# Five matmuls per fp32r weight tile in the feed-forward, in place of six

## What is computed

```python
def rmsnorm(x, g):
    y = xf * lax.rsqrt(jnp.mean(xf * xf, axis=-1, keepdims=True) + EPS)
    return (y * g).astype(x.dtype)

def swiglu(h, w_gu, w_down):
    gate, up = jnp.split(h @ w_gu, 2, axis=-1)
    return (jax.nn.silu(gate) * up) @ w_down

def layer(...):
    x = x + 0.5 * swiglu(rmsnorm(x, n1), ffn1_gu, ffn1_down)
    h = rmsnorm(x, n_mix)
    ...            # projections, gated linear attention and window attention
    x = x + jnp.concatenate([o_g, o_s], axis=-1) @ w_out
    x = x + 0.5 * swiglu(rmsnorm(x, n2), ffn2_gu, ffn2_down)
```

## Time and profile before

| | |
|---|---|
| median of 3 runs | 2183.99 us (2182.62 to 2188.75) |
| span of the profiled execution | 2178.1 us |
| what lies between the two | 5.9 us |
| TensorE matmul busy | 2116.3 us, 97% |
| VectorE, ScalarE, GpSimd busy | 811.9, 581.5, 800.7 us |

### The profile page before, as it was taken

One profiled execution on the slowest core, in us unless ns is written; L12 is line 12 of the kernel. 1 busy time (PEld: TensorE's weight loads), 2 busy tenths in 40 slices (PEclk: granted clock), 3 DMA queues, 4 the chain that ended last, 5 costly groups with the idle time before them and its releaser, 6 DMA issues.

```text
span 2178.1 us, 40378 instructions
## 1 busy us (share of the span) xinstructions
PE 2116.3 (97%) x16718; PEld 2078.8 (95%) x16718; DVE 811.9 (37%) x1125; ACT 581.5 (27%) x795; POOL 800.7 (37%) x337
## 2 busy tenths in 40 slices
PE   6999999999999999999999999999999999999996
PEld 6999999998889999999999999999898999999996
DVE  5222222486257222222332222226754452222224
ACT  3222222235233222222232222222532322222222
POOL 3333344432113333344433333444221233444443
PEclk9999999999889999999999999999997999999998
DMA  4222222421212222222222222233221122222222
GB/s 137 90 87 87 87 87 97 132 78 50 81 51 78 87 88 88 88 93 97 89 87 87 87 88 88 96 96 123 69 90 39 61 88 87 87 87 87 92 92 99
DMA packets 56869, 190.53 MB, mean 87 GB/s; under 512 B 8976, under 2 KB 10672, under 8 KB 56240
## 3 DMA queue, kind: packets, MB, share of 16 engines
q1 hardware_dynamic: 48960, 176.31, 25.0%
q10 hardware_dynamic: 7824, 13.00, 1.8%
HBM read 184.37 MB, written 6.95 MB: 88 GB/s over the span
## 4 chain that ended last, share of the span: by engine, by line
PE 92%; DVE 6%; issue 1%; ACT 0%; DMA 0%; DVEq 0%; ACTq 0%
PE ps L379 84%; DVE h_hi L989 2%; PE ps L538 1%; DVE ssum L1003 1%; PE ps L651 1%; PE ps L527 1%; DVE h_lo L992 1%; PE ps L444 1%; PE ps L645 1%; PE ps L690 1%; PE ps L718 0%; PE ps L510 0%; DVE x L1323 0%; PE ps L679 0%; PE ps L704 0%
## 5 line engine op out<-in xcount | busy, mean ns | idle before, releaser
L366 POOL TENSOR_TENSOR w_lo<-w_raw,w_hi 128x1024 fp32r<-128x1024 f32 x332 | 800.3, 2411 | 1359.4 <-ACT w_hi L745 1345.2
L379 PE MATMUL ps<-h_hi,w_hi 128*128 128x272 f32 x3424 | 718.8, 291 | 23.8 <-DVE h_lo L992 22.1
L379 PE MATMUL ps<-h_lo,w_hi 128*128 128x272 f32 x3424 | 712.9, 290 | 0.0
L379 PE MATMUL ps<-h_hi,w_lo 128*128 128x272 f32 x3424 | 710.8, 289 | 0.0
L745 ACT ACTIVATE w_hi<-w_raw 128x1024 fp32r<-128x1024 f32 x328 | 347.5, 1060 | 1349.2 <-PE ps L379 1349.1
L379 PEld LDWEIGHTS ps<-h_hi,w_hi 128*128 128x128 f32 x3424 | 544.1, 190 | 28.8 <-issue 24.8
L379 PEld LDWEIGHTS ps<-h_hi,w_lo 128*128 128x128 f32 x3424 | 543.4, 190 | 0.0
L379 PEld LDWEIGHTS ps<-h_lo,w_hi 128*128 128x128 f32 x3424 | 538.9, 190 | 0.0
L379 PE MATMUL ps<-act_lo,w_hi 128*128 128x272 f32 x1408 | 291.6, 289 | 0.0
L379 PE MATMUL ps<-act_hi,w_hi 128*128 128x272 f32 x1408 | 291.2, 288 | 0.0
L379 PE MATMUL ps<-act_hi,w_lo 128*128 128x272 f32 x1408 | 290.4, 288 | 0.0
(11 more groups left out here) (213 smaller groups left out, 1246.8 us busy)
## 6 DMA issues: line engine op xcount, KB each, us to landing
w_raw<-stream SPq DMA_DIRECT2D x332, 512.0 KB, 3.4
x<-xT ACTq DMA_DIRECT2D x8, 272.0 KB, 6.3
y_d<-x SPq DMA_DIRECT2D x8, 272.0 KB, 2.1
s<-s_d ACTq DMA_DIRECT2D x2, 1024.0 KB, 4.9
s_s_d<-s ACTq DMA_DIRECT2D x2, 1024.0 KB, 4.6
kc<-kc_d ACTq DMA_DIRECT2D x2, 512.0 KB, 5.2
vc<-vc_d ACTq DMA_DIRECT2D x2, 512.0 KB, 6.6
k_s_d<-kc_d ACTq DMA_DIRECT2D x2, 496.0 KB, 8.9
```

The costliest lines, as they stand in the source:

```text
L366: pool.tensor_tensor(w_lo[:, q, :], w_raw[:, q % RAW, :], w_hi[:, q, :].bitcast(F32), ALU.subtract).then_inc(lo_ready, 1)
L379: ins = pe.matmul(dst[:, hf, :], w[:, slot, cols], r[:, hf * TH:(hf + 1) * TH], start=first and w is w_hi and r is rhs_hi, stop=last and r ...
```

## The change

In the feed-forward alone, the moving operand of a weight tile is laid out as one row of 1088 columns: high half 0, the first 90 low columns of half 0, high half 1, the first 90 low columns of half 1, and the other 2 x 182 low columns. `wide_product` runs w_hi over it in three matmuls of 362, 362 and 364 columns, and w_lo over the two high halves in two of 272. The three w_hi matmuls write three PSUM banks (a `tri`), with the low products beside the high ones; they are added on the way out. So an output tile takes three banks and only two are in the air (six banks; the last two serve the norm). The evacuation becomes: ScalarE copies the low columns out (`copy_low`, two instructions), VectorE adds the high columns (`add_high`), then scales in SBUF. ScalarE also makes the high part of h (`high_h`) and of act (`high_act`). The head of a feed-forward half is written anew: the first two tiles run over seven k, then their last k, then `norm_sum`, then the third tile, which needs the first tile's banks.

```diff
+TAIL = 90
+REST = TH - TAIL
+HW = TH + TAIL
+TW = 2 * T
...
+        def tri(i):
+            return ps[:, 3 * i:3 * i + 3, :]
...
+            def wide_product(dst, slot, col, r, first, last):
+
+                cols = slice(col, col + P)
+                for hf in range(2):
+                    pe.matmul(dst[:, hf, 0:HW], w_hi[:, slot, cols], r[:, hf * HW:(hf + 1) * HW],
+                              start=first, stop=False)
+                pe.matmul(dst[:, 2, 0:2 * REST], w_hi[:, slot, cols], r[:, 2 * HW:TW], start=first, stop=last)
+                for hf in range(2):
+                    ins = pe.matmul(dst[:, hf, 0:TH], w_lo[:, slot, cols], r[:, hf * HW:hf * HW + TH],
+                                    start=False, stop=last)
+                return ins
...
-                pe.wait_ge(h_ready, hb + 5)
-                for q in range(4):
-                    if q == 3:
-                        pe.wait_ge(norm_root, l * 3 + (half * 2 + 1))
-                    model_tile(pair(q), ch + q, q, hb if q == 0 else None).then_inc(chunk_done, 1)
-                    if q == 0:
-                        norm_sum(l * 3 + half * 2)
+                pe.wait_ge(h_ready, hb + (1 if half == 0 else 6))
+                pe.wait_ge(down_used, l * (2 * KT) + (half * KT + 1))
+                for q in range(2):
+                    pe.wait_ge(lo_ready, ch + (q + 1 + RING))
+                    if q:
+                        pe.wait_ge(h_ready, hb + (KT - 1))
+                        pe.wait_ge(down_used, l * (2 * KT) + (half * KT + 2))
+                    for k in range(KT - 1):
+                        if q == 0:
+                            pe.wait_ge(h_ready, hb + (k + 1))
+                        wide_product(tri(q), q, k * P, hx[:, k, :], k == 0, False)
+                pe.wait_ge(h_ready, hb + KT)
+                for q in range(2):
+                    wide_product(tri(q), q, (KT - 1) * P, hx[:, KT - 1, :], False, True).then_inc(chunk_done, 1)
+                norm_sum(l * 3 + half * 2, 3)
+                for q in range(2):
+                    pe.wait_ge(up_used if q else gate_summed, fb + 1)
+                    wide_tile(tri(q), ch + (2 + q), 2 + q).then_inc(chunk_done, 1)
...
+            def high_h(n, gain, wide):
+
+                act.activation(high_cols(hx[:, n, :]) if wide else mid_cols(hx[:, n, :])[0],
+                               halves(x[:, n, :]), ACT.Copy, scale=gain).then_inc(h_high, 1)
+
+            def copy_low(dst, src, done):
+
+                act.wait_ge(chunk_done, done + 1)
+                d = low_pieces(dst)
+                act.activation(d[0], src[:, 0:2, TH:HW], ACT.Copy)
+                act.activation(d[1], halves(src[:, 2, 0:2 * REST]), ACT.Copy).then_inc(low_copied, 1)
...
-                high_part(chunk(l, c0 + RING), 0)
-                root(l * 3 + half * 2)
-                for q in range(1, 4):
-                    high_part(chunk(l, c0 + RING + q), q)
+                for q in range(4):
+                    c = chunk(l, c0 + RING + q)
+                    copy_low((a_buf if q % 2 else g_buf)[:, q // 2, :], tri(q % 2), c[0])
+                    high_part(c, q)
+                    if q == 1:
+                        root(l * 3 + half * 2)
+                        silu(fb, 0)
+                    elif q == 2:
+                        silu(fb + 1, 1)
                     if q % 2:
-                        silu(fb + q // 2, q // 2)
+                        high_act(fb + q // 2, q // 2, q // 2)
...
+            def add_high(dst, src, count):
+
+                dve.wait_ge(low_copied, count)
+                return dve.tensor_tensor(halves(dst), src[:, 0:2, 0:TH], halves(dst), ALU.add)
...
                 scale_ready(l * 3 + half * 2)
                 with dve.Fori(0, FT // 2) as i:
                     for q in range(2):
+                        dve.wait_ge(chunk_done, i * 4 + (cb + 2 * q + 1 + RING))
+                        add_high(g_buf[:, q, :], tri(0), i * 4 + (wb + 2 * q + 1)).then_inc(gate_summed, 1)
+                        dve.wait_ge(gate_summed, i * 2 + (fb + q + 1))
                         if q == 0:
                             dve.wait_ge(rs_ready, l * 3 + (half * 2 + 1))
...
                 def evacuate(n):
                     dve.wait_ge(chunk_done, cb + (CH_GU + DN_CH * (n + 1) + RING))
-
-                    dve.scalar_tensor_tensor(out=halves(a_buf[:, n % 2, :]), in0=pair(n % 4), scalar=0.5,
-                                             in1=halves(rs[:, :]), op0=ALU.mult,
-                                             op1=ALU.mult).then_inc(down_used, 1)
-                    dve.wait_ge(down_used, l * (2 * KT) + (half * KT + n + 1 + 4))
+                    add_high(a_buf[:, n % 2, :], tri(n % 2), wb + CH_GU + n + 1).then_inc(down_used, 1)
+                    dve.wait_ge(down_used, l * (2 * KT) + (half * KT + n + 1 + 2))
+
+                    dve.scalar_tensor_tensor(out=a_buf[:, n % 2, :], in0=a_buf[:, n % 2, :], scalar=0.5,
+                                             in1=rs[:, :], op0=ALU.mult, op1=ALU.mult).then_inc(down_scaled, 1)
+                    dve.wait_ge(down_scaled, l * (2 * KT) + (half * KT + n + 1))
                     dve.tensor_tensor(x[:, n, :], x[:, n, :], a_buf[:, n % 2, :], ALU.add).then_inc(x_ready, 1)
```

More of the change, by code:

```diff
@@ L258, in pair, with high_cols, low_cols, mid_cols @@
             return ps[:, 2 * i:2 * i + 2, 0:TH]
+        def tri(i):
+            return ps[:, 3 * i:3 * i + 3, :]
+        def high_cols(ap):
+            return ap[:, 0:2 * HW].rearrange("p (h n) -> p h n", h=2)[:, :, 0:TH]
+        def low_cols(ap):
+            return (ap[:, 0:2 * HW].rearrange("p (h n) -> p h n", h=2)[:, :, TH:HW],
+                    ap[:, 2 * HW:TW].rearrange("p (h n) -> p h n", h=2))
+        def mid_cols(ap):
+            q = ap.rearrange("p (h c n) -> p h c n", h=2, c=2)
+            return q[:, :, 0, :], q[:, :, 1, :]
+        def low_pieces(ap):
+            two = ap if len(ap.shape) == 3 else halves(ap)
+            return two[:, :, 0:TAIL], two[:, :, TAIL:TH]
         def halves(ap):
@@ L387, in model_tile, with wide_tile, norm_sum @@
                 for k in range(KT):
-                    if hb is not None and k >= 5:
+                    if hb is not None and k >= 7:
                         pe.wait_ge(h_ready, hb + (k + 1))
-                    ins = product(dst, slot, k * P, h_hi[:, k, :], h_lo[:, k, :], k == 0, k == KT - 1)
+                    ins = product(dst, slot, k * P, *mid_cols(hx[:, k, :]), k == 0, k == KT - 1)
                 return ins
-            def norm_sum(phase):
+            def wide_tile(dst, chunk, slot):
+                pe.wait_ge(lo_ready, chunk + (1 + RING))
+                for k in range(KT):
+                    ins = wide_product(dst, slot, k * P, hx[:, k, :], k == 0, k == KT - 1)
+                return ins
+            def norm_sum(phase, at):
                 pe.wait_ge(ssum_ready, phase + 1)
-                square_sum(pair(3), ssum).then_inc(norm_summed, 1)
+                square_sum(pair(at), ssum).then_inc(norm_summed, 1)
             def ffn_half(l, half):
@@ L436, in output_half @@
                         pe.wait_ge(m["mix_ready"], half * 4 + k + 1)
-                    ins = product(dst, c % RING, (n % 2 * 4 + k) * P, *mixed(half * 4 + k),
+                    ins = product(dst, c % RING, (n % 2 * 4 + k) * P, *map(halves, mixed(half * 4 + k)),
                                   k == 0, k == 3)
@@ L983, in rope_swap, with new_h @@
                 return [8 + i if i < 8 else i - 8 if i < 16 else i for i in range(32)]
-            def new_h(n, gain, step, squares):
-                dve.tensor_scalar(h_hi[:, n, :], x[:, n, :], gain, None, ALU.mult).then_inc(h_step, 1)
-                k = n + max(n - 2, 0) + 1
-                dve.wait_ge(h_step, step + k)
-                dve.scalar_tensor_tensor(out=h_lo[:, n, :], in0=x[:, n, :], scalar=gain,
-                                         in1=h_hi[:, n, :].bitcast(F32), op0=ALU.mult,
-                                         op1=ALU.subtract).then_inc(h_ready, 1)
+            def new_h(n, gain, wide, adds, squares):
+                dve.wait_ge(h_high, squares + n + 1)
+                his = low_pieces(high_cols(hx[:, n, :]).bitcast(F32)) if wide else \
+                    (mid_cols(hx[:, n, :])[0].bitcast(F32),)
+                los = low_cols(hx[:, n, :]) if wide else (mid_cols(hx[:, n, :])[1],)
+                xs = low_pieces(x[:, n, :]) if wide else (halves(x[:, n, :]),)
+                for lo, hi, src in zip(los, his, xs):
+                    ins = dve.scalar_tensor_tensor(out=lo, in0=src, scalar=gain, in1=hi, op0=ALU.mult,
+                                                   op1=ALU.subtract)
+                ins.then_inc(h_ready, 1)
                 if n >= 2:
-                    add_square(n - 1, squares + n, h_step)
+                    if n >= 3:
+                        dve.wait_ge(sq_added, adds + (n - 2))
```

(3 more changed lines are left out.)

108 lines of the change are left out of this document (66 added, 42 removed).

## The result

The changed kernel takes 2236.07 us (median of 4 runs, 2234.78 to 2237.7), the kernel before 2184.82 beside it: a ratio of 1.0243, with a 95% interval of 1.0231 to 1.0255. It is 51 us slower. The forecast said 2196, at most 2232: the sign was right and the size was not. Of all the runs quoted in this document one, of the kernel with the later weight chunk, was slow at 5272.67 us: its median is over all four runs, its ratio over the other three.

What follows compares the result with a forecast made beforehand. The prediction took TensorE's unbroken matmul runs as the bound, with other engines counting only at heads and boundaries. Terms -25 + 40 - 9 + 6 = +12 us on 2178.1 gave 2190, with 5.9 around it 2196 us; range 2165 to 2232.

Steps and rivals of the forecast that it cites:

- Term 1: Feed-forward matmuls: one fewer per weight tile saves a fixed 12.0 ns, -25.2 us, with 0 and -82 as ends.
- rival 2: Feed-forward matmuls: cost is a pure rate per column, so nothing is saved there; 2221 us, chance 0.19.
- rival 3: Feed-forward matmuls: fixed part only 3.3 ns as for fp32 records, the rest a rate; 7 saved, 2214 us, chance 0.11.
- rival 1: Feed-forward matmuls: the weight load is the limit, hidden under longer matmuls; -82 us, total 2139, chance 0.13.
- Term 2: Heads of feed-forward halves: third tile waits for the high add behind the reciprocal, then low clock; +40 us, bounds 25 and 48.
- Term 3: Heads and program start: seven-k cover, ScalarE's high parts and an earlier TensorE start gain; -9 us, bounds 0 and -14.
- Term 4: Boundaries into the mixer and the end: add to x meets GpSimd, 2.1 us later each; +6 us, bounds 0 and +9.
- Rival 5: Gate and up loop: VectorE waits for GpSimd, 0.25 us per tile, 44 us more; 2240 us, chance 0.03.

Runs made afterwards that it cites:

- the kernel with the later weight chunk: Changed kernel with ScalarE making a down tile's last weight chunk after the high part of h and the square: 2228.84 us, ratio 1.0199.
- the pattern with 240: Changed kernel with 240 instead of 90 columns per half in the third bank, so wide matmuls of 512 columns: 2401.75 us, one run.
- the run with the reciprocal late: Changed kernel with VectorE's first gate and up high adds of each half put ahead of the reciprocal: 2196.0 us, ratio 1.0052.
- the second run with matmuls behind the end: Changed kernel plus unused matmuls after its last norm, five column patterns from own starts and from row starts; some 1000 us more expected, time no measure.

## Why the prediction was right or wrong

**Term 1, the failed step.** "I take the fixed part", 12.0 ns for each matmul of whatever length, was the step that failed. The 12.0 ns are what six matmuls of 272 columns spend beside their columns. The five of the change spend (754.3 - 680.0) / 5 = 14.9 ns, or 16.0 in the half of 1150 us; those with 88 or 92 columns 12.0, with 80 columns 12.7 or 10.7. A half has 528 weight tiles, so the term was not -25.2 but 528 x (3 x 2.6 + 8.3) ns = +8 us, 33 us off. The pure rate (rival 2) and the 3.3 ns (rival 3) would have come nearer, 2221 and 2214, for a reason that is wrong as well: with 88 columns the saving is there, 35 us against 90, and the forecast's 740 ns a weight tile with it. That the load is no limit (against rival 1) held: no tile of this kernel came near 713 ns. My bounds for the term were 0 and -82; below nothing I had excluded a loss without any row that excludes it, since no row of before has another length than 272 at full clock in fp32r.

The Trainium skill, page "TensorE: Matmul & The Clock Gate", section "Back-to-back issue gap", has about 2.5 ns beside the columns. The prediction applied it to a stream; the section itself gives it for a matmul by itself and has other figures for streams of loads and matmuls, about 131 ns at 512 columns. Neither agrees with fp32r here: no stretch in the loop or alone had a mean under 9.3 ns beside the columns, and 512 columns took 227.5 ns alone and 238 in the pattern with 240.

**Term 2 was right.** 33 us of stall forecast, 28.5 there (7.83, 6.42, 7.85, 6.42); 7 of clock forecast, 8.6 there. Sum forecast 40, there 37, and taking it away gave 40 with the boundaries' clock. The order of the chain, and the table load that is absent after the mixer, were as said.

**Term 3 failed,** a smaller step: -9 us forecast and -0.5 found, of three parts.

At the start, -5 forecast, +2.9 found: without the stall the third tile starts at 39.09 (the run with the reciprocal late), before at 36.19. "It could begin at about 11 and have both first tiles done near 29": the first matmul came at 12.92, but the last h only at 30.6 and the two tiles ended at 38.4. ScalarE's copy for h stands behind its wait for a sum of squares on VectorE, so the two engines take turns and VectorE waits 0.82 us at most tiles; and VectorE met GpSimd in the low part where it had met it in the high one. The larger part is in the program and in the clock: the second tile waits for the seventh h, which came at 28.35, and behind that stand ten weight tiles, 7.5 us at 754 ns, so 29 could not be met. They took 10.03, as the first of them ran at 1.2 GHz, behind a stretch in which TensorE had waited for each h. Timeline of ScalarE, then of TensorE, then the windows view of 30 to 40 us:

```profile
16.84 0.75 ACT L823 ACTIVATE hx<-x,g_first 128x544 fp32r<-128x544 f32 x1 [3.08 <-DVE ssum L1104]
...
28.35 0.97 PE L419 MATMUL ps<-hx,w_hi 128*128 128x362 f32 x2 [1.97 <-DVE hx L1091]
...
30.00:40.00 10.00, 9.46 (x50) 8.95 (x48) 2.02 (x4) 3.72 (x8) 0.47 (x1) 0.82 0.06 22
```

After the mixer, 2 x -0.9 forecast, 2 x -1.7 found: from its last matmul to the norm's sum 12.19 us for 7.79, with one tile of 6.0 more in between. Between two feed-forward halves, -2 forecast, nothing found (14.13 for 8.17, one tile more): the old 1.76 us are gone, but TensorE now waits as long for the high add of the last down tile, since that frees its banks:

```profile
1121.89 0.57 PE L419 MATMUL ps<-hx,w_hi 128*128 128x362 f32 x2 [1.71 <-DVE a_buf L1109]
```

**Term 4** forecast 2.1 us a boundary and an add to x of over 2 us: it took 2.81. The norm's sum begins 1.7 us later behind the last matmul at each boundary into the mixer (8.4 for 6.7), and the end comes 1.8 later: 5.2 us for the 6 forecast. The low clock behind these two boundaries adds 1.6 each, which the forecast did not have; the norm's sum takes 2.18 and 1.84 us there, where the earlier trace rows has 1.19. The Trainium skill, page "SBUF — State Buffer", section "Who interferes with whom", names the contention; 2.81 us beside GpSimd and 0.72 without agree.

**The sum:** 2196 + 33 + 9 = 2238 by the two repaired terms, 2236 measured. In the two traces the terms are +8, +37, -0.5 and +8.4, so 53 of the 57.8 us; the other 4 are in the mixers, as said above. That the first sum comes within 2 us is in part luck. Rival 5 did not come: no wait for VectorE inside the loop in any of the four feed-forward runs. The range ended at 2232 because term 1 ended at 0, and its +8 lies outside.

**What stays open:** why a pattern of lengths and starts costs 10.7 or 16 ns a matmul. The times of the steady patterns are near a grid: 733.3, 740.0, 753.3, 760.0 and 833.3 ns are 110, 111, 113, 114 and 125 times 6.667 ns, which is 16 cycles of 2.4 GHz; 743.3 is half-way, and 754.3 and 751.7 are not on it. That is a reading of numbers and no mechanism that a run shows. What puts one half of a program at 760.0 and its neighbours at 754.3 was not tried.

## What to carry to other kernels

A saving that rests on the cost of an instruction in a length that the trace does not have should be bounded by a loss too, and the length treated as a free constant: here 88, 90, 92 and 96 columns differ by 14 ns in 740, some 30 us, and the start times in one trace of each tell them apart; a few hundred matmuls behind the program's end, with the exact lengths and starts, foretold the loop within 3 ns, apart from the second speed that some halves took. When banks are shared by fewer tiles, what frees them must not stand behind a long instruction that frees nothing: moving two adds ahead of a reciprocal of 3.55 us was worth 40 us. Moving an operation to an idle engine gained nothing here, where the next one had to wait for it and then met the same contention. And an earlier start of TensorE is worth only what stands behind the last input: here ten weight tiles stood behind the seventh h, at the low clock.

## What the runs showed of the hardware that I had not expected

- Weight tiles of five fp32r matmuls of 272 to 384 columns, back to back at full clock, take their columns and 10.7 to 16 ns a matmul more, by how lengths and starts combine; four of them came back to 0.2 ns with no other engine at work.
- The same instructions settle at one of two speeds in a stretch and keep to it for hundreds of microseconds: 754.3 or 760.0 ns with 90 columns, 743.3 or 733.3 with 80. In five traces with 90 columns the slow one came in different halves.
- 512 columns cost 25 ns beside their columns in the pattern with 240, and 14 alone.
- An idle time of 6.4 to 7.85 us is followed by 6.8 us at 1.2 GHz in all four heads of the changed kernel (10.2 us in two of the four in the second run with matmuls behind the end).
- The clock fell without a long wait too: from 20 to 28 us of the changed kernel it had matmuls in flight for 2.75 of 8 us, with no wait over 2.7 us, its clock was low from 23.5 on, and from 28 to 30 us it was 0.50.
